# Modulation vectors of a two-stream transformer block: 17 of 18 summed on VectorE, both streams packed in one tile, the last sum over partitions as split products

## The reference, cut to what matters

```python
def mod_vectors(cvec, w_mod, b_mod):
    m = jax.nn.silu(cvec) @ w_mod + b_mod          # 1024 x 9216 for each layer
    return jnp.split(m, N_MOD, axis=-1)
def sandwich_ffn(x, w_gate_up, w_down, g_pre, g_post, shift, scale, gate):
    h = modulate(rms_norm(x, g_pre), shift, scale)
    return x + 0.5 * gate * rms_norm(swiglu(h, w_gate_up, w_down), g_post)
```

## Time and profile before

| | |
|---|---|
| median of 3 runs | 2806.58 us (2806.21 to 2806.8) |
| profiled execution, its own time | 2806.0 us |
| its span | 2804.2 us |
| PE busy | 2627.1 us |
| DVE busy | 1451.4 us |
| ACT busy | 994.9 us |
| `gate_up` of F00, F01, F10, first matmul | at 64.37, 757.35, 1160.05 us |

### The profile page before, as it was taken

How to read it: one execution, slowest core, us unless ns; L and a number is a source line. 1 busy time by engine, 2 the same in 40 slices (tenths; PEclk the granted TensorE clock), 3 DMA queues, 4 the chain that set the end, 5 groups by cost and what they waited for, 6 DMA issues and landing times.

```text
span 2804.2 us, 31212 instructions
## 1 busy us (share of the span) xinstructions
PE 2627.1 (94%) x13088; PEld 2115.7 (75%) x13088; DVE 1451.4 (52%) x2189; ACT 994.9 (35%) x1455; POOL 82.6 (3%) x102
## 2 busy tenths in 40 slices
PE   5999998999699999899999898998999999988898
PEld 2777885756477888677887655996888799776897
DVE  6764444353654332775354455445465545565444
ACT  3221224243322222422223334344454444455433
POOL 0000001200100000100000110000000000000000
PEclk8999999999899999999999989998999999999999
DMA  7654343410444322454343423554544355433454
GB/s 252 210 181 135 120 134 114 119 44 31 136 144 142 105 98 98 143 175 148 108 148 105 114 86 108 171 183 148 184 154 150 120 165 181 151 121 105 151 181 143
DMA packets 240316, 385.93 MB, mean 138 GB/s; under 512 B 8628, under 2 KB 148020, under 8 KB 240112
## 3 DMA queue, kind: packets, MB, share of 16 engines
q1 hardware_dynamic: 236176, 372.43, 40.3%
q0 software_dynamic: 4000, 11.51, 1.6%
HBM read 382.81 MB, written 3.00 MB: 138 GB/s over the span
## 4 chain that ended last, share of the span: by engine, by line
PE 81%; DVE 8%; ACT 5%; issue 3%; DMA 1%; SPq 1%; POOL 0%; DVEq 0%; ACTq 0%; POOLq 0%
PE ps L503 25%; PE ps L505 24%; PE ps L504 24%; ACT hs L1109 2%; DVE wlo L1657 2%; ACT whi L1096 2%; PE ps L554 1%; PE ps L697 1%; PE ps L721 1%; DVE arena L1788 1%; DVE arena L1820 1%; PE ps L578 1%; PE ps L706 1%; DMA raw<-in_w_mod 1%; ACT Hhi L1150 1%
## 5 line engine op out<-in xcount | busy, mean ns | idle before, releaser
L1657 DVE TENSOR_TENSOR wlo<-raw,whi 128x2048 fp32r<-128x2048 f32 x279 | 637.3, 2285 | 953.6 <-ACT whi L1096 953.5
L1096 ACT ACTIVATE whi<-raw 128x2048 fp32r<-128x2048 f32 x279 | 532.4, 1909 | 1444.8 <-PE ps L505 1382.0
L503 PE MATMUL ps<-Hlo,whi 128*128 128x256 f32 (+1 forms) x2184 | 739.0, 338 | 47.4 <-DVE Hlo L1809 24.8
L504 PE MATMUL ps<-Hhi,wlo 128*128 128x256 f32 (+1 forms) x2184 | 734.8, 336 | 0.0
L505 PE MATMUL ps<-Hhi,whi 128*128 128x256 f32 (+1 forms) x2184 | 734.7, 336 | 0.0
L503 PE MATMUL ps<-wlo,Hhi 128*128 128x512 f32 x1504 | 599.7, 399 | 23.9 <-DVE Hlo L1809 12.1
L504 PE MATMUL ps<-whi,Hlo 128*128 128x512 f32 x1504 | 590.2, 392 | 0.0
L505 PE MATMUL ps<-whi,Hhi 128*128 128x512 f32 x1504 | 590.2, 392 | 0.0
L503 PEld LDWEIGHTS ps<-Hlo,whi 128*128 128x128 f32 x2184 | 418.5, 192 | 109.2 <-DVE Hlo L1809 26.3
L505 PEld LDWEIGHTS ps<-Hhi,whi 128*128 128x128 f32 x2184 | 418.0, 191 | 42.0
L504 PEld LDWEIGHTS ps<-Hhi,wlo 128*128 128x128 f32 x2184 | 418.7, 192 | 41.0
(11 more groups left out here) (250 smaller groups left out, 1636.5 us busy)
## 6 DMA issues: line engine op xcount, KB each, us to landing
raw<-in_w_ffn_gate_up SPq DMA_DIRECT2D x88, 1024.0 KB, 5.1
raw<-in_w_mod SPq DMA_DIRECT2D x65, 1024.0 KB, 5.1
raw<-in_w_ffn_down SPq DMA_DIRECT2D x44, 1024.0 KB, 4.9
raw<-in_ffn_w_in SPq DMA_DIRECT2D x44, 1024.0 KB, 5.1
raw<-in_attn_w_in SPq DMA_DIRECT2D x36, 1024.0 KB, 5.1
raw<-in_ffn_w_out SPq DMA_DIRECT2D x22, 1024.0 KB, 4.9
raw<-in_w_in SPq DMA_DIRECT2D x16, 1024.0 KB, 5.0
raw<-in_mlstm_w_in SPq DMA_DIRECT2D x12, 1024.0 KB, 5.2
```

Source lines behind the costliest of these rows:

```text
L503: e.matmul(o, L[0], R[1], start=start, stop=False)
L504: e.matmul(o, L[1], R[0], start=False, stop=False)
L1096: e.activation(hi_of(n), slot(n), ACT.Copy).then_inc(*A.up(("hi", n)))
L1657: e.tensor_tensor(lo_of(n), slot(n), hi_of(n).bitcast(F32), ALU.subtract).then_inc(*V.up(("lo", n)))
```

## The change

All vectors but (0,1) are summed on DVE; `plain` units stay for (0,1) alone, and `pre` has none. Sides lie now in `gate_up` of F00 for (0,2) to (0,6), of F01 for (0,8), (1,0), (1,1), (1,2), of F10 for (1,4) to (1,8), and in `down` of F00 for (0,7), of F01 for (1,3). Vectors 5 to 8 of layer 1 are summed for one stream. When a half is summed, DVE adds the two halves of the partitions of each stream, packs both streams in one tile of 64 + 64 partitions, and splits it into an fp32r pair in `HS` (`side_parts`). PE multiplies this pair with a small 0/1 constant: for a gate as a row (two products of 512 columns), for a shift or scale with the sums as weights, in eight products of 2 columns that land as columns, so no transposes follow. Rows of gates go to a DRAM tensor of their own each. `tick` has three steps: parts (two units after the sum), pick and take (one unit later each).

```diff
-        yield from self.finish(2)
-        if self.summed and self.count - self.summed[0][1] >= 2:
-            yield from self.finish()
-            yield self.pick()
+        for k, (step, later) in enumerate([("parts", 2), ("pick", 1), ("take", 1)]):
+            if self.summed[k] and self.count - self.summed[k][0][1] >= later:
+                what, _ = self.summed[k].pop(0)
+                if k < 2:
+                    self.summed[k + 1].append((what, self.count))
+                if k == 0:
+                    self.picked += 1
+                yield (step, *what)
...
+        for k, step in enumerate(("parts", "pick", "take")):
+            while self.summed[k]:
+                what = self.summed[k].pop(0)[0]
+                if k == 0:
+                    self.picked += 1
+                    for s in ("parts", "pick", "take"):
+                        yield (s, *what)
...
+SIDE = {(0, 0): [(0, 2), (0, 3), (0, 4), (0, 5), (0, 6)], (0, 1): [(0, 8), (1, 0), (1, 1), (1, 2)],
+        (1, 0): [(1, 4), (1, 5), (1, 6), (1, 7), (1, 8)]}
+SIDE_DOWN = {(0, 0): (0, 7), (0, 1): (1, 3)}
...
+    return 1 if l and v >= 5 else 2
...
-        push(("mod", l, 5), "plain", 2 if l else None)
...
-        push(("mod", l, 8), "plain")
...
                     if what == "pick":
-                        fill = ("pick", l, v, h)
+                        fill, pk = ("pick", l, v, h), pickr[:, 2 - streams(l, v), :]
                         b = bank(fill)
-                        w.wait_ge(*LD["cst"].at("cst"))
+                        w.wait_ge(*A.at("pickr"))
                         w.wait_ge(*V.at(("side", l, v, h)))
-                        for s in range(2):
-                            i = e.matmul(b[0:2, :], cs("pick")[:, 2 * s:2 * s + 2], acc[acc_of[l, v, h] % 2][s],
-                                         start=s == 0, stop=s == 1)
+                        if v in GATE:
+                            e.matmul(b[0:2, :], pk, HS[0], start=True, stop=False)
+                            i = e.matmul(b[0:2, :], pk, HS[1], start=False, stop=True)
+                        else:
+                            for k in range(4):
+                                o, c = b[:, 2 * k:2 * k + 2], slice(128 * k, 128 * k + 128)
+                                e.matmul(o, HS[0][:, c], pk, start=True, stop=False)
+                                i = e.matmul(o, HS[1][:, c], pk, start=False, stop=True)
...
-                mod_steps([("pick", 0, 0, h)])
-                feed.summed.clear()
-            vector_turn(0, 0)
+                mod_steps(feed.every())
...
+                    w.wait_ge(*T.at(("pick", 0, 0, 1)))
...
+            def side_parts(l, v, h):
+
+                a0, a1 = acc[acc_of[l, v, h] % 2]
+                w.wait_ge(*V.at(("sum", l, v, h, 7, streams(l, v) - 1)))
+                if streams(l, v) == 2:
+                    e.tensor_tensor(a0[0:64, :], a0[0:64, :], a0[64:128, :], ALU.add).then_inc(
+                        *V.up(("half", l, v, h, 0)))
+                    w.wait_ge(*V.at(("half", l, v, h, 0)))
+                    e.tensor_tensor(a0[64:128, :], a1[0:64, :], a1[64:128, :], ALU.add).then_inc(
+                        *V.up(("half", l, v, h, 1)))
...
+                e.tensor_copy(HS[0], a0).then_inc(*V.up(("shi", l, v, h)))
+                w.wait_ge(*V.at(("shi", l, v, h)))
+                e.tensor_tensor(HS[1], a0, HS[0].bitcast(F32), ALU.subtract).then_inc(*V.up(("side", l, v, h)))
```

More of the change, by code:

```diff
@@ L113, in __init__ @@
         self.hold, self.until = False, 8
-        self.sums, self.picked, self.summed, self.rest = 0, 0, [], []
+        self.sums, self.picked, self.summed = 0, 0, [[], [], []]
     def unit(self):
@@ L143, in due @@
             yield n
[L145 to L154, removed]
-    def tick(self):
-        yield from self.finish(2)
-        if self.summed and self.count - self.summed[0][1] >= 2:
-            yield from self.finish()
-            yield self.pick()
-    def every(self):
-        while self.summed:
-            yield self.pick()
-        yield from self.finish()
+    def tick(self):
+        for k, (step, later) in enumerate([("parts", 2), ("pick", 1), ("take", 1)]):
[6 more added lines that the diff above has]
+                yield (step, *what)
+    def every(self):
+        for k, step in enumerate(("parts", "pick", "take")):
[6 more added lines that the diff above has]
+                else:
+                    yield (step, *what)
+                    if k == 1:
+                        yield ("take", *what)
 GATE = {2: (1, True), 5: (3, False), 8: (5, True)}
+GATES = [(l, v) for l in range(2) for v in GATE]
 PRE_GAIN = {1: 0, 4: 2, 7: 4}
@@ L253, in weight_stream, with push_down @@
             stream.append(side_src(0, 1, h, u) + ("plain", None))
+    def push_down(w, key=None):
+        for j, u in enumerate(units_of(("out", w, NF))):
+            stream.append(u + ("cut", None))
+            if key in SIDE_DOWN and j in (1, 3, 5, 7):
+                what = (*SIDE_DOWN[key], (j - 1) // 4, (j - 1) // 2 % 2)
+                stream.append(side_src(*what) + ("side", what))
     for l in range(2):
         push_gu(gu1[l, 0], (l, 0))
[L256 to L260, removed]
-        push(("mod", l, 5), "plain", 2 if l else None)
+        push_down(dn1[l, 0], (l, 0))
         for g in MIX_ORDER:
@@ L290, in weight_stream @@
     order = [n for n in range(len(stream)) if stream[n][3] != "side"]
[L291 to L298, removed]
+    return stream, order, at
 def build(nc, a, out):
@@ L607, in gate_up @@
                         mod_steps(feed.tick())
-                assert not feed.summed and not feed.rest
+                assert not any(feed.summed)
             def out_product(P, nk, left):
@@ L1178, in pre @@
             def pre(P):
-                gate = GATES.get(P)
-                halves = gate[2] if gate else 0
                 parts = []
@@ L1193, in pre @@
                     hi_part(*parts.pop(0))
-                for _ in range(2 * halves):
-                    through()
                 feed.hold, feed.until = False, len(units)
@@ L1589, in scalar_program @@
             H_FREE["F00"] = A.at("sc")
+            hs_pick = {"F00": ("pick", 0, 6, 1), "F01": ("pick", 1, 2, 1), "F10": ("pick", 1, 8, 1)}
             H_FREE["M1"] = T.at(("y", "F10", 3))
```

187 lines of the change are left out of this document (83 added, 104 removed).

## The result

| | before | after |
|---|---|---|
| median | 2806.69 us (4 runs, 2806.21 to 2808.11) | 2846.7 us (4 runs, 2844.04 to 2849.6) |
| ratio, 95 % interval | | 1.0142 (1.0124 to 1.0159) |
| span of the profiled execution | 2804.2 us | 2842.2 us |
| PE busy / DVE busy | 2627.1 / 1451.4 us | 2569.6 / 1555.1 us |

What follows compares the result with a forecast made beforehand. PE, with 81 % of the chain, bounds the kernel; DVE's work is free only while PE need not wait. Terms for `gate_up`, start, `pre`, M0, M1 and clock sum to +18.6 on 2806.0: 2824.6 us, range 2810 to 2842.

Steps and rivals of the forecast that it cites:

- The clock term: Places with 5 to 12 us of new wait: PE's products run at half level briefly, net +2.0 us (0 to 8).
- the rival in which the short waits cost clock too: Much slower: clock falls at each wait, 19 waits of 1.7 us more in place of 2.0, 2855 us; chance 0.08.
- The waits of F10: F10 `gate_up`: waits of 0.8, 5.2, 1.9 and 0.9 us, none from (1,5) on; stage +2.6 us.
- the whole stage: F00 `gate_up`: waits 24.7 and 5.6 us, picks 8.0 against 18.0 before; +20.3 us.
- `pre` of F01: First product at 741.4, when the normalised tile is ready, in place of 757.35: -15.9 us.
- The steady step: `gate_up`: split ready 12.3 us after PE's unit against 10.88, so PE waits 1.4 us a pick.
- The start: Splits and picks of both halves come ahead of the second plain half, which is copied at 51.65: +12.1 us.
- M0: First projection of M0: DVE cuts, then splits and picks follow in turn until 513.1: +6.0 us.
- `pre` of M0 and F11: The wait for the gate row goes in M0, -3.9 us; a wait of 4.54 goes in F11, -6.0 us.
- The picks: On PE: 0.65 us for a gate, 0.9 for a shift or scale, against 2.03 before plus 0.58 a turn.
- The transposes' row: Lower end for a shift or scale pick on PE: eight small transposes, 0.62 us.
- The faster rival: DVE is in time: `gate_up` stages gain -10.0, -5.1 and -6.2 us, the rest -14.0; 2771 us, chance 0.07.

Runs made afterwards that it cites:

- The filler: The changed kernel with six idle products of 512 columns on PE ahead of each pick in F01 `gate_up` alone: 2841.8 us, 1.0128.
- The combined kernel: The changed kernel with take and parts first in `gate_up`, plain units first at the start, (0,7)'s splits early, M0's side sum behind `pre`: 2768.3 us, 0.9873.
- both first: The changed kernel with DVE's take and parts ahead of the next cut and side sums in `gate_up`: 2796.8 us, ratio 0.9967.
- the old pick: The changed kernel's weight stream and sides, with pick, row, turns and start order of the kernel before, no `parts`: 2815.9 us, 1.0036.
- the two combined kernels: The changed kernel with all order moves together, 2768.3 us, and the same with the rope table behind F00 `gate_up`, 2767.7 us.

## Why the prediction was wrong, step by step

**The clock term failed.** "Net +2.0 (0 to 8)", for long waits alone; the slow products of the three stages rose by 6.3 + 4.1 + 9.7 = 20.1 us. I had seen slow products only behind waits of 3.9 us and more, and gave the rival in which the short waits cost clock too a chance of 0.08 with 32 us in it. The filler shows that this rival's mechanism is real: the seven waits of 1.54 us cost 4.4 us in F01. Its size was too large for F01 and F00 (1.7 us for each of 19 waits): in F01 two stretches of 1.7 us followed seven short waits, in F00 none followed the last three. In F10 it was right: behind five of the six waits, those of 1.17 and 1.64 us too, stands a slow stretch that cost 1.6 to 2.6 us (behind 8.24 us of wait the unit lasts 12.6 us, from 1252.64 to the pick, in place of 10.9).

**The waits of F10 failed.** I had 8.8 us, and from (1,5) on no wait at all; 19.9 were there. The forecast followed one chain, from sum to split to pick, and let `take` and the reading of `HS` cost nothing. The trace has both on the path: PE's cut unit waits for the bank of a pick, the cast for PE. In F00 one of the three long waits (7.57 us) is of this kind too, so its 23.8 us, against 30.3 forecast, came about in another way than I laid out: 6.1 and 4.4 us at the first two picks (6.8 and 6.4 forecast), then the bank, then three steady ones. That the whole stage came to +21.5 against +20.3 was luck: 6.5 us less of waits, 6.3 more of slow products, and picks that gained 8.5 and not 10.0.

**`pre` of F01** gained 12.0 of 15.9: that the normalised tile would be ready at 741.4 took for granted that nothing else moves ahead of it. The plain units had also held back the next side sum; shown by holding it back again.

**What held.** The steady step: 1.54 us a pick against 1.4, seven times in F01 (the 4.4 us that I gave its first pick were 1.54 too); `parts` 2.59 us against 2.68, the cast 0.43, under the 0.48 that I took. The start (+13.0 against +12.1) and M0 (+7.8 against +6.0) by the very chain that was written down, though the picks at these places took 1.8 us each and not 1.1 and 1.0; `pre` of M0 and F11 to 0.2 us; M1. The picks gained 8.5, 4.8 and 5.5 us (forecast 10.0, 5.1, 6.2). A pick for a shift lasts eight times 0.11 us, 0.9 as I took it. The transposes' row would have been the wrong price. They load 128 columns as well, but of two rows, and follow each other every 0.062 us in the traces; the new picks load 128 columns of 128 rows, every 0.11. The Trainium skill (TensorE: Matmul & The Clock Gate, LDWEIGHTS) gives columns/1.2 ns for a load, 107 ns for 128 columns, however many rows it has: this agrees with the 0.11 and not with the 0.062.

**The faster rival** named 2771 us for splits that are ready in time. The change had not that in it. The combined kernel took 2768, but that the two agree is luck. The rival had -21.3 us for the three `gate_up` stages, -14.0 for the rest; measured against before, the combined kernel has +8.6, -6.0 and -2.4 in F00, F01 and F10 `gate_up`, and the rest comes from the start and M0, in whose order the rival had changed nothing, and from M0's clock. With both first alone it took 2797. What was right is the mechanism in F01, where no pick waits once the split stands ahead; and the point from which it decides was one of order as well as of 1.4 us of work.

**Not explained.** Behind F11, where nothing was changed, the profiled execution after is 8.8 us shorter. The attention stage there took 274.6 us before and 271.7 after, at a granted clock of 0.99 and 1.00, and over all profiles it is one or the other, some 274.5 in four (with the old pick, with both moved first, and in the two combined kernels) beside before, 271.7 in the rest. All of these 2.9 us stand in one stretch of the same 201 PE instructions, before and after:

```profile
1936.07:1993.99 57.92, 45.62 (x201) 38.24 (x200) 30.30 (x55) 28.12 (x48) 2.52 (x2) 0.85 0.41 136
1981.89:2036.91 55.02, 42.43 (x201) 35.83 (x200) 30.25 (x55) 28.17 (x48) 2.52 (x2) 0.91 0.43 143
```

The larger part lies in the last stages. From the first product of F11 on every kernel has the same 6120 PE instructions; they take 1052.7 us before, 1052.1 and 1052.4 in the two combined kernels, 1050.8 with both first, 1046.6 with the old pick and 1044.0 to 1045.2 in the others. Whether a kernel or an execution sets which was not tried. Without these 8.8 us the change would have cost 47 and not 38, and differences of a few us between the totals of two kernels say little unless the stages say the same.

## What to carry to other kernels

When work moves to an engine with time to spare, look at where it stands in that engine's program, not at its share: the same instructions in another order were worth 50 us here. Follow every resource that the new step holds (a bank until it is taken, a tile until it is read), and each one that the removed step held back. And where the bound engine has a clock that falls when it idles, a wait can cost more than its length; here repeated short ones did too.

## What the runs showed of the hardware that I had not expected

Behind two of F01's seven waits of 1.54 us, which stand some 24 us apart, PE's products ran at half speed (0.43 us for 512 columns instead of 0.23) for some eight products; behind a wait of 1.17 us in F10 (at 1364.27) they did so too. Filling F01's waits with idle products removed this (7.4 to 3.0 us of slow products in 263 us, granted clock 0.98 to 0.99). At the lower level a pick of eight small products takes 1.7 us (0.21 each, as at 35.51 and 538.90) instead of 0.9. And the same instructions can run at another granted clock in two kernels that differ elsewhere: 100 PE instructions of M0 took 25.8 us at 1.00 or 30.7 at 0.78.
